# First expert's rows placed by products instead of fetched by index: a decoder layer with two-level expert routing on one core

## The chip, the core and the metric

One core of a Trainium2 chip runs the whole kernel. The metric is the device time of one execution in microseconds (us). Everything is float32. Tiles have 128 partitions (rows of tokens, or slices of the model width). TensorE is called PE below, its weight loads PEld, VectorE DVE, ScalarE ACT, GpSimd POOL, and SyncE SP (it issues the weight transfers).

## The reference, cut to what matters

One layer on 512 prompt tokens and 64 sample tokens (576 rows of width 1024): conditioning, a mixing sub-layer (attention and a gating MLP, one output projection), then the expert sub-layer. Only the seam between the last two is touched:

```
x  = x + ga1 * rms_norm(mix @ w_out, g_post_mix)
h2 = rms_norm(x, g_pre_ffn) * (1 + sc2) + sh2                # 576 x 1024
g_logits = h2 @ w_rg + b_rg                                  # 4 groups: the largest wins
e_logits = h2 @ w_re + b_re                                  # 4 experts in it: the two largest win
y = sum over the 16 experts e of gate[:, e] * (silu(h2 @ w_gate[e]) * (h2 @ w_up[e])) @ w_down[e]
x = x + ga2 * rms_norm(y, g_post_ffn)
```

## The kernel before, in words

The stage that matters is `merge`, followed by `experts`. `merge` goes over five token tiles, in the order `ORDER`: four of 128 prompt rows (tiles 0 to 3) and one of 64 sample rows (tile 4). Before, the order is 0, 1, 2, 4, 3. For each tile PE multiplies the turned mix by the output projection (L2011, two halves of 512 columns; L2019 for the sample tile); ACT sums squares of the result; POOL makes the reciprocal root (L1603 to L1606 for the last tile); DVE adds to x (L1841, L1843 for the last tile), ACT and POOL do the same for the second norm, and DVE makes the normed rows `h2` (L1848, L1849). ACT stores `h2` in memory (L1673, L1691). PE turns `h2` and multiplies it by the router's 20 columns (L1985). The last tile's logits are made from `x` itself, turned (L2038) and multiplied by pre-scaled router columns (L2049), so that they need not wait for `h2`.

Routing is done on DVE by `route(t0, t1)` for the tiles t0 to t1-1: a chain of short instructions (L1749 to L1770), each waiting for the one before. Tiles 0 to 2 are routed while PE still multiplies the last tile; tiles 3 and 4 (the function is called with 3 and 5) come after the last tile's logits. PE counts, for each chosen expert, the rows ahead of each row (`RANK`, products with a triangular and an all-ones matrix: L1969 to L1973 for three tiles, L2054 to L2057 for two). The function `first` turns the ranks for expert 0 into a one-hot matrix `first_row` that says which place each token takes in expert 0's tile of 128 rows. PE multiplies that by the token numbers (L2043, L2061), DVE casts the result into an index list (L1876), and POOL issues an indirect transfer that gathers 128 rows of `h2` from memory (`gather(0)`, L2179). PE turns them (L2322, the function `tokens`), ACT and DVE copy them out of PSUM (L2202, L2079), and the first expert begins.

Each expert is a gate product (L2350, 16 passes of PE over 512 columns), an up product (L2360, 16 passes), the turn of its hidden rows (L2415) and, one expert later, a down product (L2385). PE's order there is gate(e), up(e), tokens(e+1), down(e-1), turn(e). All other lists of rows come from `table` (L2332), which PE runs between gate(0) and up(0) and for which DVE must have finished a long chain (L1877 to L1920); its result is cast at L1922, and POOL then issues `gather(1)` and `gather(2)`. The weights live in a ring of eight slots of 2 MB that SP fills in order; a slot is free again once PE has used it. Expert 0's three and expert 1's gate weights are requested before `merge` begins, expert 1's up and down weights once the output projection is done (L1482), all later ones after DVE has sorted the experts by load (L1924 to L1928, `order_done`).

Of the kernel before, what the change touches and what calls it, by code (L numbers as in the profile page):

```python
# [56 lines left out]
ORDER = (0, 1, 2, 4, 3)  # L57
# [13 lines left out]
def rows(t):  # L71

    return P if t < 4 else NS
# [149 lines left out]
class Program:  # L223
# [1262 lines left out]
    def merge(self, block):  # L1486
# [20 lines left out]
        hv = [L.at(L.V + D * i, D) for i in range(2)]  # L1507
# [27 lines left out]
        both = hot_all[:, 160:256]  # L1535
# [20 lines left out]
        first_row = L.at(L.HT, NT * P).rearrange("p (t c) -> p t c", t=NT)  # L1556
# [23 lines left out]
        def _(sp):  # L1580
# [7 lines left out]
            self.load_expert(sp, 1, 1, 0)  # L1588
            sp.wait_ge(proj_done, 4)
            self.load_expert(sp, 1, 1, 1)  # L1590
            self.load_expert(sp, 1, 1, 2)

        @block.gpsimd
        def _(pool):
            link = chain(pool, pchain, self.pool_count)
            for i, t in enumerate(ORDER):
                n = rows(t)
                for s, first, ready, done in ((ss1, ss1a, sq1, rs1), (ss2, ss2a, sq2, rs2)):
                    pool.wait_ge(ready, i + 1)
                    if i < END:  # L1600
                        self.power(pool, link, s[:, t:t + 1], 1, n, 1.0 / D, done)
                    else:
                        link(pool.tensor_scalar(first, first, 1.0, D * EPS, ALU.mult, ALU.add))  # L1603
                        pool.wait_ge(ready, i + 2)
                        link(pool.tensor_scalar(s[:, t:t + 1], s[:, t:t + 1], first, 1.0 / D, ALU.add, ALU.mult))
                        pool.tensor_tensor(s[:, t:t + 1], s[:, t:t + 1], L.cst("half", n)[:, 0:1], ALU.pow  # L1606
                                           ).then_inc(done, 1)
                if i == 1:
                    pool.wait_ge(ss_ready, 1)
                    self.power(pool, link, ss8, H, NS, 1.0 / DV, ss_power)  # L1610

        @block.scalar
        def _(act):
# [26 lines left out]
            act.dma_start(self.x1[:, 0, :], x_of[0]).then_inc(x_in[0], 16)  # L1640
# [3 lines left out]
            for t in range(1, NT):  # L1644
# [10 lines left out]
            for i, t in enumerate(ORDER[:END]):  # L1655
# [5 lines left out]
                if i >= 2:  # L1661
                    act.wait_ge(h2_tr, i - 1)
                    act.wait_ge(h2_out2[i % 2], 16 * (i // 2))
                act.activation(hv[i % 2][0:n], proj(i, n), ACT.Square, accum_out=ss1[0:n, t:t + 1]).then_inc(sq1, 1)
# [5 lines left out]
                act.activation(hv[i % 2][0:n], self.x1[0:n, t, :], ACT.Square,  # L1670
                               accum_out=ss2[0:n, t:t + 1]).then_inc(sq2, 1)
                act.wait_ge(h2_done, i + 1)
                act.dma_start(self.h2[P * t:P * t + n, :], hv[i % 2][0:n]).then_inc(h2_out2[i % 2], 16)  # L1673
# [1022 lines left out]
```

## Time and profile before

| what | value |
|---|---|
| three runs | 880.01, 882.63, 885.31 us; median 882.63 us |
| the profiled execution | 884.13 us, of which the span of all instructions is 882.4 us |
| PE busy | 811.1 us, 92% of the span |
| mean granted clock of PE | 0.964 of 2.4 GHz |
| last output projection product ends | 534.5 us after the start of the span |
| first expert's gate product begins | 559.28 us |

The span is the time from the first instruction to the last; 1.7 us lie around it. Times of instructions are counted from the start of the span. A line number names a line of the kernel before; where a number of the changed kernel is meant, the text says so. A product in float32 appears as two records ("passes") for each matmul; a turn (transpose) as one. A granted clock of 1.00 is 2.4 GHz, one of 0.50 is 1.2 GHz.

### The profile page before, as it was taken

The numbers are of one execution on the slowest core, as the hardware profiler recorded it, in microseconds if no ns is written. First come the engines' busy times: TensorE is split into PE (matmuls) and PEld (weight loads), VectorE is DVE, ScalarE is ACT, GpSimd is POOL, SyncE is SP. The second block draws the span as 40 slices with busy tenths as digits, with TensorE's granted clock in tenths as the row PEclk, the third lists the DMA queues.
The fourth block names the chain that finished last, engine by engine and source line by source line (L and its number), as shares of the span: only waits on it lengthen the run. The fifth ranks groups of instructions, "written<-read, shape, count | busy, mean of one in ns | idle before, by whom it ended". The sixth has DMA issues, their size and how long they took to land. (4 is left out here: it accounts for less than half of the span.)

```text
span 882.4 us, 12191 instructions
## 1 busy us (share of the span) xinstructions
PE 811.1 (92%) x4728; PEld 411.1 (47%) x4728; DVE 341.6 (39%) x839; ACT 200.2 (23%) x425; POOL 120.5 (14%) x192
## 2 busy tenths in 40 slices
PE   4599999999999999999788987799999999999994
PEld 3144344444446666665544555444444444444431
DVE  3213162346668755555414675510031011110146
ACT  4001000244455433433202111111011110110132
POOL 2220010300002222221101101100000000000044
PEclk8899999999999999999999987799999999999998
DMA  8998194740005979996989515198889999999882
GB/s 295 392 275 355 64 414 136 269 148 2 13 13 209 378 303 425 424 428 283 405 309 329 222 36 215 34 401 330 336 318 408 423 392 426 393 393 387 328 276 107
DMA packets 37142, 249.18 MB, mean 282 GB/s; under 512 B 4809, under 2 KB 6217, under 8 KB 23650
## 3 DMA queue, kind: packets, MB, share of 16 engines
q1 hardware_dynamic: 23490, 156.35, 45.3%
q0 software_dynamic: 9376, 81.47, 23.6%
q10 hardware_dynamic: 4224, 10.65, 3.8%
q8 instruction: 35, 0.57, 0.3%
q14 instruction: 17, 0.14, 0.0%
HBM read 231.92 MB, written 16.53 MB: 282 GB/s over the span
## 5 line engine op out<-in xcount | busy, mean ns | idle before, releaser
L2360 PE MATMUL ps<-sb 128*128 128x512 f32 (+1 forms) x256 | 112.9, 594 | 0.0
L784 PE MATMUL ps<-sb 128*128 128x512 f32 x192 | 86.4, 604 | 1.8 <-DVE sb L442 1.8
L2284 DVE TENSOR_TENSOR sb<-sb,ps 128x512 f32<-128x512 f32 (+1 forms) x16 | 10.9, 684 | 160.3 <-PE ps L2360 87.1
L2350 PE MATMUL ps<-sb 128*128 128x512 f32 x144 | 65.8, 611 | 1.0 <-ACT sb L2202 0.9
L1161 PE MATMUL ps<-sb 128*128 128x128 f32 x512 | 62.9, 276 | 1.8 <-ACT sb L1260 1.8
L2011 PE MATMUL ps<-sb 128*128 128x512 f32 x128 | 59.1, 622 | 4.8 <-ACT sb L1619 2.8
L2385 PE MATMUL ps<-sb 128*128 128x512 f32 x144 | 63.5, 594 | 0.0
L1161 PEld LDWEIGHTS ps<-sb 128*128 128x128 f32 x512 | 55.4, 140 | 13.3 <-issue 10.0
L1064 PE MATMUL ps<-sb 128*128 128x512 f32 x128 | 59.2, 597 | 0.3 <-DVE sb L969 0.3
L2360 PEld LDWEIGHTS ps<-sb 128*128 128x128 f32 (+1 forms) x256 | 42.0, 167 | 34.0 <-issue 34.0
L784 PEld LDWEIGHTS ps<-sb 128*128 128x128 f32 x192 | 36.2, 193 | 45.5 <-issue 43.9
L2357 PE MATMUL ps<-sb 128*64 128x512 f32 x112 | 49.6, 595 | 0.0
L1303 DVE COPY sb<-ps 128x512 f32<-128x512 f32 x64 | 41.2, 686 | 21.6 <-PE ps L1161 21.6
L2179 POOL DMA_INDIRECT sb<-h_rows,ints x16 | 15.0, 940 | 238.6 <-PE ps L2322 209.5
L943 ACT ACTIVATE sb<-sb 128x128 f32<-128x128 f32 (+3 forms) x64 | 35.4, 554 | 52.4 <-DVE sb L1027 52.4
L2350 PEld LDWEIGHTS ps<-sb 128*128 128x128 f32 x144 | 27.4, 195 | 33.1 <-issue 31.2
L2011 PEld LDWEIGHTS ps<-sb 128*128 128x128 f32 x128 | 25.2, 200 | 35.8 <-issue 32.7
L1027 DVE CUSTOM_DVE_ANT_0 sb<-ps,sb 128x128 f32<-128x128 f32 (+3 forms) x64 | 28.8, 488 | 32.9 <-PE ps L1099 29.3
L2385 PEld LDWEIGHTS ps<-sb 128*128 128x128 f32 x144 | 26.7, 190 | 30.3 <-issue 30.1
L2295 DVE COPY sb<-ps 128x512 f32<-128x512 f32 (+1 forms) x16 | 11.1, 692 | 75.8 <-PE ps L2385 56.2
L1260 ACT ACTIVATE sb<-ps 128x512 f32<-128x512 f32 x64 | 34.7, 592 | 21.8 <-PE ps L1161 19.8
L1400 PE MATMUL ps<-sb 128*32 128x512 f32 (+1 forms) x320 | 36.6, 530 | 2.5 <-DVE sb L1347 1.6
(346 smaller groups left out, 1036.2 us busy)
## 6 DMA issues: line engine op xcount, KB each, us to landing
sb<-in_w_gate SPq DMA_DIRECT2D x16, 2048.0 KB, 19.5
sb<-in_w_up SPq DMA_DIRECT2D x16, 2048.0 KB, 9.7
sb<-in_w_down SPq DMA_DIRECT2D x16, 2048.0 KB, 14.3
sb<-in_w_ada SPq DMA_DIRECT2D x12, 2048.0 KB, 18.8
sb<-in_w_in SPq DMA_DIRECT2D x5, 2048.0 KB, 22.1
y_rows<-sb SPq DMA_DIRECT2D x9, 512.0 KB, 15.5
sb<-in_w_out SPq DMA_DIRECT2D x2, 2048.0 KB, 24.2
sb<-in_x_prompt SPq DMA_DIRECT2D x4, 512.0 KB, 5.4
```

What stands on the lines that cost most here:

```text
L784: last = pe.matmul(PS[:, n % 4, :], L.hT[:, k, t * P:t * P + P], w[:, k, :], start=k == 0, stop=k == KC - 1)
L943: act.activation(pb[n % 3][j][:, 0:w], pb[n % 3][j][:, 0:w], ACT.Exp, bias=nm[:, q:q + 1], scale=-1.0, accum_out=sums[:, q:q + 1]).then_in ...
L1064: last = pe.matmul(PS[:, bank, :], L.hT[:, k, t * P:t * P + P], w[:, k, :], start=k == 0, stop=k == KC - 1)
L1161: last = pe.transpose(self.PS[:, h, P * g:P * g + P], kp[:, 4 * (ch % 2) + g, P * h:P * h + P], self.L.cst("ident"))
L1260: act.activation(kt[ch % 2][:, h, :], PS[:, h, :], ACT.Copy).then_inc(kt_act, 1)
L1303: dve.tensor_copy(kt[ch % 2][:, h, :], PS[:, h, :]).then_inc(kt_dve, 1)
L1400: last = pe.matmul(bank[32 * h:32 * h + 32, 0:512 if ch < 4 else NS], qst[par][:, h, :], rhs, start=True, stop=True)
L2011: last = pe.matmul(PS[:, proj_bank(i, c), :], mixT[i % 2][:, k, :], w[:, k, :], start=k == 0, stop=k == KC - 1)
L2350: last = pe.matmul(PS[:, 0, :], x[:, k, :], w_gate[:, k, :], start=k == 0, stop=k == KC - 1)
L2357: last = pe.matmul(PS[n:P, 0, :], x[:, k, :], w_gate[:, k, :], start=k == 0, stop=k == KC - 1)
L2360: last = pe.matmul(PS[0:n, 1, :], x[:, k, :], w_up[:, k, :], start=k == 0, stop=k == KC - 1)
L2385: last = pe.matmul(PS[:, 5 + c, :], hT[:, k, :], w[:, k, 512 * c:512 * c + 512], start=k == 0, stop=k == FC - 1)
```

## The change

Five things are done together.

1. The order of the tiles becomes 1, 2, 3, 4, 0. Tiles 1, 2, 3 are routed together while PE multiplies the last tile's projection, and the sample tile (4) by itself right after them. Only tile 0 is left for the chain behind the last logits; with one tile several pairs of instructions in `route` become one. For that the sample tile's turn, its logits and the ranks of tiles 1 to 3 are put in among the last tile's projection products on PE.
2. Expert 0's rows are no longer gathered. The normed rows of all five tiles stay on chip (in the ring slot of expert 1's gate weights, and one more buffer), and PE multiplies each by its placing matrix `first_row` (the new function `choose_rows`): 8 products of 128 columns for each tile, added up in two PSUM banks that are first set to zero by two products with zero weights. The sum is expert 0's input, already turned. For this the places of expert 0 are now counted from tile 1 on, with tile 0 last.
3. What is gathered by ranks is now expert 1's rows: a second one-hot matrix `second_row` (640 columns), five products with the token numbers, one cast, `gather(1)`.
4. `table` moves from between gate(0) and up(0) to between gate(1) and up(1); its first row list is then expert 2's. The sort of the experts (`order_done`) moves ahead of the long chain on DVE.
5. Expert 1's gate weights are requested after the last placing product, as their slot holds the normed rows until then. The last tile's `h2` is made by a product with the scale first and then one instruction with the reciprocal root, in place of the root first.

The diff, cut to its core:

```diff
-ORDER = (0, 1, 2, 4, 3)
+ORDER = (1, 2, 3, 4, 0)
@@ merge
-        hv = [L.at(L.V + D * i, D) for i in range(2)]
+        held = expert_slot(1, 0)[0]
+        hv = [L.ring[held][:, D * i:D * i + D] for i in range(NT - 1)] + [L.at(L.V, D)]
@@ merge, SP
             for kind in range(3):
                 self.load_expert(sp, 0, 0, kind)
-            self.load_expert(sp, 1, 1, 0)
             sp.wait_ge(proj_done, 4)
             self.load_expert(sp, 1, 1, 1)
             self.load_expert(sp, 1, 1, 2)
+            for out in h2_out2:
+                sp.wait_ge(out, 32)
+            sp.wait_ge(self.x_tr, self.up(self.x_tr, 1))
+            self.load_expert(sp, 1, 1, 0)
@@ merge, DVE
-            route(0, 3)
+            route(1, 4)
+            link(dve.tensor_reduce(three, both[:, 16:64]..., AX, ALU.add))
+            read_logits(END - 1)
+            route(4, NT)
+            dve.tensor_tensor(four, three, both[:, 64:80], ALU.add).then_inc(hot_done, 1)
+            first(1, 4, 1)
...
-            read_logits(i - 1)
-            first(0, 3)
-            dve.wait_ge(rs2, NT)
+            first(4, NT, 2)
             dve.wait_ge(x1_done, NT + 1)
-            link(dve.scalar_tensor_tensor(h, x1, ss2[:, t:t + 1], mod[1], ALU.mult, ALU.mult))
-            dve.tensor_tensor(h, h, mod[2], ALU.add).then_inc(h2_done, 1)
+            link(dve.tensor_tensor(h, x1, mod[1], ALU.mult))
+            dve.wait_ge(rs2, NT)
+            dve.scalar_tensor_tensor(h, h, ss2[:, t:t + 1], mod[2], ALU.mult, ALU.add).then_inc(h2_done, 1)
...
-            route(3, NT)
+            route(0, 1)
...
+            first(0, 1, 3)
+            dve.tensor_copy(ranks[:, 16:96], RANK[:, 16:96]).then_inc(rank_read, 1)
+            dve.tensor_copy(ranks[:, 0:16], RANK[:, 96:112]).then_inc(rank_read, 1)
+            link(dve.scalar_tensor_tensor(rk.unsqueeze(2), rank[:, :, 1:2], 1.0, hot[:, 2, :, 1:2], ALU.add, ALU.mult))
+            dve.scalar_tensor_tensor(second_row, L.cst("row")..., 1.0, rk..., ALU.add, ALU.is_equal).then_inc(first_done, 1)
...
-            dve.tensor_copy(self.ints[:, 0:1], PS[:, 0, 0:1]).then_inc(self.first_ready, 1)
+            dve.tensor_copy(self.ints[:, 1:2], PS[:, 7, 200:201]).then_inc(self.first_ready, 1)
@@ merge, PE
+            def choose_rows(i, ks):
+                t = ORDER[i]
+                n = rows(t)
+                if i == END:
+                    pe.wait_ge(h2_done, NT)
+                for k in ks:
+                    last = pe.matmul(PS[:, 4 * (k // 4), (k % 4) * P:(k % 4) * P + P], hv[i][0:n, k::KC],
+                                     first_row[0:n, t, :], start=False, stop=i == END and k % 4 == 3)
+                return last
...
+                            if (i, f, k) == (END, 1, 2):
+                                logits_of(END - 1)
+                            if (i, f, k) == (END, 1, 4):
+                                ranks_of_three()
                         if i == END and f == 0:
                             last.then_inc(halves, 1)
+                            h2_tr_of(END - 1)
...
-            pe.wait_ge(first_done, 1)
-            for t in range(3):
-                pe.matmul(PS[:, 0, 0:1], first_row[:, t, :], L.cst("token")[:, t:t + 1], start=t == 0, stop=False)
...
+            choose_rows(1, range(KC))
+            choose_rows(2, range(KC))
+            pe.wait_ge(first_done, 2)
+            choose_rows(3, range(KC))
+            pe.wait_ge(hot_done, 4)
+            pe.matmul(RANK[:, 96:112], L.cst("before"), both[:, 0:16], start=False, stop=False)
+            pe.matmul(RANK[:, 80:96], L.cst("ones"), both[:, 0:16], start=False, stop=True).then_inc(rank_done, 1)
+            pe.wait_ge(first_done, 3)
+            choose_rows(END, range(KC)).then_inc(self.x_tr, 1)
+            pe.wait_ge(first_done, 4)
+            for t in range(NT):
+                last = pe.matmul(PS[:, 7, 200:201], second_row[0:n, t, :], L.cst("token", n)[:, t:t + 1],
+                                 start=t == 0, stop=t == NT - 1)
@@ experts, POOL
+            pool.wait_ge(x_tr, self.up(x_tr, 1))
-            gather(0)
+            gather(1)
             pool.wait_ge(self.table_done, 1)
-            for e in range(1, MAIN):
+            for e in range(2, MAIN):
@@ experts, PE
-                if e == 0:
+                if e == 1:
                     table()
...
-            tokens(0, 0, P)
```

PE around the last tile's second projection half, before. L2011 is the projection, L1961 the sample tile's turn, L1969 to L1973 the ranks of three tiles, L1985 the sample tile's logits, L2038 the turn of the last tile's x:

```order
L2011 MATMUL ps<-sb 128x512 [waits e_x1]
L2011 MATMUL ps<-sb 128x512 x7
L1961 MATMUL ps<-sb 128x64 [waits e_h2_ev_dve,e_h2_ev,e_h2]
L1961 MATMUL ps<-sb 128x64 x7
L1969 MATMUL ps<-sb 128x48 [waits e_hot]
L1970 MATMUL ps<-sb 128x32
L1971 MATMUL ps<-sb 128x16
L1973 MATMUL ps<-sb 128x48 x3
L1985 MATMUL ps<-sb 64x20 [waits e_h2_ev_dve,e_h2_ev]
L1985 MATMUL ps<-sb 64x20 x7
```

The same place in the changed kernel, where L2043 is the projection, L1986 the turn, L2017 the logits, and L1994 to L1996 the ranks:

```order
L1986 MATMUL ps<-sb 128x64 [waits e_h2_ev_dve,e_h2_ev,e_h2]
L1986 MATMUL ps<-sb 128x64 x7
L2043 MATMUL ps<-sb 128x512 [waits e_x1]
L2043 MATMUL ps<-sb 128x512 x2
L2017 MATMUL ps<-sb 64x20 [waits e_h2_ev_dve,e_h2_ev]
L2017 MATMUL ps<-sb 64x20 x7
L2043 MATMUL ps<-sb 128x512 x2
L1994 MATMUL ps<-sb 128x48 [waits e_hot]
L1995 MATMUL ps<-sb 128x32
L1996 MATMUL ps<-sb 128x16
L2043 MATMUL ps<-sb 128x512 x3
```

What stood behind the projection now stands inside it, ahead of its last products.

PE from the last tile's logits to the first expert's gate product, before (L2049 the logits, L2054 to L2057 the ranks of two tiles, L2061 the index list, L2322 the turn of the gathered rows, L2350 the gate product):

```order
L2049 MATMUL ps<-sb 64x20 [waits e_h2_ev]
L2049 MATMUL ps<-sb 64x20 x7
L2054 MATMUL ps<-sb 128x32 [waits e_hot]
L2055 MATMUL ps<-sb 128x32
L2057 MATMUL ps<-sb 128x16
L2061 MATMUL ps<-sb 128x1 [waits e_first]
L2061 MATMUL ps<-sb 128x1
L2313 UNCONDITIONAL_BRANCH
L2322 MATMUL ps<-sb 128x128 [waits vs_out]
L2322 MATMUL ps<-sb 128x128 x7
L2350 MATMUL ps<-sb 128x512 [waits ring_full4,ident_in,half_set]
```

The same in the changed kernel (L2093 the logits, L2006 the placing products, L2102 and L2103 the ranks of tile 0, L2109 the index list, L2401 the gate product):

```order
L2093 MATMUL ps<-sb 64x20 [waits e_h2_ev]
L2093 MATMUL ps<-sb 64x20 x7
L2006 MATMUL ps<-sb 128x128 x16
L2006 MATMUL ps<-sb 128x128 [waits e_first]
L2006 MATMUL ps<-sb 128x128 x7
L2102 MATMUL ps<-sb 128x16 [waits e_hot]
L2103 MATMUL ps<-sb 128x16
L2006 MATMUL ps<-sb 128x128 [waits e_h2,e_first]
L2006 MATMUL ps<-sb 128x128 x7
L2109 MATMUL ps<-sb 128x1 [waits e_first]
L2109 MATMUL ps<-sb 128x1 x4
L2365 UNCONDITIONAL_BRANCH
L2401 MATMUL ps<-sb 128x512 [waits ring_full4,cols_in,cols_tr]
```

24 placing products now stand between the logits and the ranks, 8 more and the index list behind them; the gather and the turn of its rows are gone.

## Rows read from the trace of the kernel before

**Rows 1.** Waits of PE, 470 to 560 us: total, times, longest
```profile
PE ps L2054 <- DVE sb L1770: 5.0, 1, 5.0
PE ps L2322 <- DMA sb<-h_rows,ints: 4.9, 1, 4.9
```
**Rows 2.** Chain that ended last, 541 to 578 us: start, us, what
```profile
542.38 1.22 DVE sb L1849
...
543.79 0.17 DVE sb L1754
...
552.09 4.29 DMA sb<-h_rows,ints
...
556.42 1.98 PE ps L2322 x8
...
559.28 8.92 PE ps L2350 x16
...
570.44 7.06 PE ps L2360 x16
```
**Rows 3.** Windows: busy PE, PEld, DVE, ACT, POOL, granted clock, DMA share, GB/s
```profile
534.50:539.00 4.50, 4.18 (x41) 3.83 (x40) 3.02 (x5) 1.79 (x5) 1.17 (x3) 1.00 0.77 255
539.00:541.40 2.40, 2.15 (x12) 2.12 (x12) 1.24 (x5) 1.78 (x4) 1.07 (x3) 0.51 1.02 437
559.28:563.00 3.72, 3.72 (x5) 1.66 (x6) 3.30 (x8) 1.04 (x1) 0.00 (x0) 0.51 0.00 0
580.00:858.00 278.00, 276.26 (x921) 121.61 (x920) 41.26 (x86) 36.02 (x64) 21.02 (x22) 0.99 0.95 374
```
**Rows 4.** Timeline of PE at the projection's end: start, us, engine, line, records
```profile
534.43 1.09 PE L1961 MATMUL ps<-sb 64*128 64x64 f32 x8
536.15 0.85 PE L1973 MATMUL ps<-sb 128*128 128x48 f32 x6
537.96 0.72 PE L2038 MATMUL ps<-sb 128*128 128x128 f32 x4
540.16 1.28 PE L2043 MATMUL ps<-sb 128*128 128x1 f32 x6
541.37 1.90 PE L2049 MATMUL ps<-sb 128*64 128x20 f32 x32
```
**Rows 5.** Timeline of ACT and DVE: a wait, last evacuation, end of routing, one-hot matrix
```profile
535.56 0.42 DVE L1715 COPY sb<-ps 128x256 f32<-128x256 f32 x1 [7.91 <-PE ps L1961]
539.86 1.15 ACT L1688 ACTIVATE sb<-ps 128x512 f32<-128x512 f32 x2
548.01 0.19 DVE L1770 TENSOR_TENSOR sb<-sb 128x32 f32<-128x32 f32 x1
549.96 0.43 DVE L1781 SCALAR_TENSOR_TENSOR sb<-sb 128x256 f32<-128x256 f32 x1
```
**Rows 6.** Timeline: eight turns of 128 columns at clock 1.00
```profile
577.35 1.04 PE L2322 MATMUL ps<-sb 128*128 128x128 f32 x8
```
**Rows 7.** Timeline of DVE: first and last of the table's chain, and of the sort
```profile
551.72 0.16 DVE L1877 TENSOR_SCALAR sb<-sb 128x16 f32<-128x16 f32 x1
558.49 0.69 DVE L2079 COPY sb<-ps 128x512 f32<-128x512 f32 x1 [0.96 <-PE ps L2322]
562.68 0.10 DVE L1920 MEMSET sb<- 64x52 f32 x1
570.58 0.42 DVE L1924 TENSOR_TENSOR sb<-sb 128x256 f32<-128x256 f32 x1
573.38 0.17 DVE L1936 CAST ints<-sb 128x11 int32<-128x11 f32 x1
```
**Rows 8.** Gathers of `h2` rows issued at 570.94, 572.22 and 578.66: us to landing
```profile
DMA to landing us min/median/max: 4.2/11.4/11.7
```
**Rows 9.** Weight transfers of SP: first of two at 534.5, last of four at 577.7
```profile
DMA to landing us min/median/max: 7.9/7.9/7.9
DMA to landing us min/median/max: 24.7/24.7/24.7
```

More of the change, by code:

```diff
@@ L1506, in merge @@
         sq = L.at(L.QKT + 4096, 512, 0, NS)
-        hv = [L.at(L.V + D * i, D) for i in range(2)]
+        held = expert_slot(1, 0)[0]
+        hv = [L.ring[held][:, D * i:D * i + D] for i in range(NT - 1)] + [L.at(L.V, D)]
+        squares = [L.at(L.V + D + 512 * i, 512) for i in range(2)]
+        rank_read = self.later("rank_read")
         osb = L.at(L.V + 2048, 512, 0, NS)
@@ L1534, in merge @@
         hot = hot_all[:, 0:240].rearrange("p (j t e) -> p j t e", j=3, t=NT)
-        both = hot_all[:, 160:256]
+        both = hot_all[:, 160:240]
+        three, four = hot_all[:, 240:256], take("four", NE)
         prod = take("prod", 80).rearrange("p (t e) -> p t e", t=NT)
@@ L1595, in _ @@
             link = chain(pool, pchain, self.pool_count)
-            for i, t in enumerate(ORDER):
+            for i, t in enumerate(ORDER[:END]):
                 n = rows(t)
-                for s, first, ready, done in ((ss1, ss1a, sq1, rs1), (ss2, ss2a, sq2, rs2)):
+                for s, ready, done in ((ss1, sq1, rs1), (ss2, sq2, rs2)):
                     pool.wait_ge(ready, i + 1)
[L1600 to L1607, printed above, removed]
+                    self.power(pool, link, s[:, t:t + 1], 1, n, 1.0 / D, done)
                 if i == 1:
@@ L1610, in _ @@
                     self.power(pool, link, ss8, H, NS, 1.0 / DV, ss_power)
+            t = ORDER[END]
+            for s, first, ready, done in ((ss1, ss1a, sq1, rs1), (ss2, ss2a, sq2, rs2)):
+                pool.wait_ge(ready, NT)
+                link(pool.tensor_scalar(first, first, 1.0, EPS, ALU.mult, ALU.add))
+                pool.wait_ge(ready, NT + 1)
+                link(pool.tensor_scalar(s[:, t:t + 1], s[:, t:t + 1], first, 1.0, ALU.add, ALU.mult))
+                pool.tensor_tensor(s[:, t:t + 1], s[:, t:t + 1], L.cst("half")[:, 0:1], ALU.pow).then_inc(done, 1)
         @block.scalar
@@ L1643, in _ @@
             act.dma_start(mod[2], row_of(3)).then_inc(mod_in, 16)
-            for t in range(1, NT):
+            for t in ORDER[1:]:
                 act.dma_start(self.x1[0:rows(t), t, :], x_of[t]).then_inc(x_in[t], 16)
@@ L2027, in _ @@
                     mix_tr(i + 1)
-                else:
-                    ranks_of_three()
-                if i >= 1:
+                if 1 <= i < END:
                     logits_of(i - 1)
+            pe.wait_ge(first_done, 1)
+            pe.wait_ge(hot_done, 3)
+            pe.matmul(RANK[:, 64:80], L.cst("before"), both[:, 64:80], start=True, stop=False)
+            pe.matmul(RANK[:, 64:80], L.cst("ones"), three, start=False, stop=True)
+            pe.matmul(RANK[:, 80:112], L.cst("ones"), four.unsqueeze(1).to_broadcast([P, 2, 16]),
+                      start=True, stop=False).then_inc(rank_done, 1)
+            for b in (0, 4):
+                pe.matmul(PS[:, b, :], L.cst("sameseq")[NS:P, 0:1].to_broadcast([P - NS, P]),
+                          L.cst("ident")[NS:P].unsqueeze(1).to_broadcast([P - NS, 4, P]), start=True, stop=False)
+            choose_rows(0, range(4))
             pe.wait_ge(h2_ev, END)
@@ L2040, in _ @@
                 last.then_inc(h2_tr, 1)
[L2041 to L2043 removed]
+                if f == 0:
+                    choose_rows(0, range(4, KC))
             pe.wait_ge(log_read, END)
```

147 lines of the change are left out of this document (76 added, 71 removed).

## The prediction, made before the changed kernel was run

> **What bounds the kernel now.** I read the busy shares in long windows first. From 580 to 858 us PE is busy 276.26 of 278.00 us at a granted clock of 0.99 [rows 3]: the experts are a plain stream of products, and no transfer, copy or other engine is waited for there. The change leaves the number and size of those products as they are, so it can move the end only by moving the start of that stream or by opening a hole in it. The waits of PE before it come next: between 470 and 560 us it waits 5.0 us for the end of routing (L1770) and 4.9 us for the gathered rows [rows 1]. The chain that ended last tells what lies between: the end of the last tile's `h2` (L1849, to 543.60), routing from 543.79, the gather at 552.09 (4.29 us), eight turns (1.98 us), their copy out of PSUM, the gate product at 559.28 [rows 2]. Last I looked at the clock. It fell at 539.0 us, although PE was busy 4.18 of the 4.50 us before, with turns and narrow products; it stayed at 1.2 GHz through the routing and came back at 563.0, after 3.7 us of products 512 columns wide [rows 3]. The first gate product therefore takes 8.92 us where the up product takes 7.06 [rows 2]: 1.9 us lost.
>
> **The change part by part**, in times of the profiled execution. Its span is 882.4 us, its own time 884.13, and it ran 1.50 us above the median of the three runs; I make the sum against 884.13 and take 1.50 off at the end.
>
> *The projection ends later.* The sample tile's turn, the ranks of three tiles and the logits stand inside the projection. Before they ran from 534.43 to 537.96, with 0.77 us for L1973, whose 0.85 us overlap the next record a little and which goes [rows 4]: 3.53 - 0.77 = +2.7 us. Their inputs are early, so no wait is added. Everything behind (squares, root, the sum with x, the turned x) moves by the same 2.7 us, as the chain ACT, POOL, DVE was what ran there and these products lay beside it.
>
> *The last logits and `h2`.* L2043 (1.28 us), which held up the logits before, is gone from there. ACT's evacuation ended at 541.01 [rows 5], now 543.7; the second half of the logits' 1.90 us [rows 4] follows it: 544.7 to 545.2. In `h2` the product with mod[1] goes ahead of the root, which takes the 1.22 us of one full-width instruction [rows 2] off the path: 543.60 + 2.7 - 1.2 = 545.1. Both meet at 545.2, and routing starts at 545.6, against 543.79: +1.8.
>
> *Routing one tile.* From L1754 at 543.79 to the end of L1770 at 548.20 there are 22 instructions [rows 2, 5], 0.20 us each. For one tile there are 18: 3.6 us, so they end at 549.2. The first three tiles and the sample tile are routed under the projection: DVE waited 7.91 us there, until 535.56 [rows 5]. The sample tile's logits arrive at about 532.5, its 19 instructions, one sum and `first` end near 537.4, and DVE's next work is at 539. That costs nothing.
>
> *The placing products are the new last wait.* Each is two passes of 128 columns, and the trace of before has none. Two rows bound a pass at full clock: a quarter of a 512-column pass (7.06 / 16 / 4 = 0.110 us) [rows 2] and a turn (1.04 / 8 = 0.130 us) [rows 6]; I take 0.122, between them, since both the columns and the weight load must fit in. At 1.2 GHz a turn takes 1.98 / 8 = 0.247 us [rows 2]. Setting the two banks to zero is 4 passes of 0.44 = 1.8 us, and tile 1's products 2.0 us: with the turned x they fill PE from 537.4 to 543.0, beside the root and the sums, and delay nothing by more than 0.2. From 545.2 PE has three tiles, 48 passes, 5.9 us: until 551.1. Routing ended at 549.2. So PE, not DVE, is late by 1.9 us. The bounds are 550.5 and 551.4. Then two rank products (0.5 us, by the 0.85 us for six passes [rows 4] and the latency of one) and `first` for 128 columns (0.45, by 0.43 for 256 columns and 0.16 for the short one ahead [rows 5]): 552.1.
>
> *From there to the gate product.* The last tile's 16 passes, 2.0 us, then the index list's 10 passes, which stand ahead of the gate product on PE: 1.28 us for six at 1.2 GHz [rows 4] makes 0.21 each there, about 0.11 at full clock, 1.1 us. The copies out of PSUM (0.88 us, from 558.40 to 559.28 [rows 2]) lie beside them. The gate product starts at 555.3, against 559.28: -4.0 us. At full clock it takes 7.0 us and not 8.92: -1.9.
>
> *DVE behind it.* The table's chain was 551.72 to 562.78, with 1.57 us for the copy L2079 and the wait ahead of it; the sort and the overflow list 570.58 to 573.55 [rows 7]. Now all of this (9.5 + 3.0 = 12.5 us) stands ahead of expert 0's hidden rows. It starts 4.4 us after `first` (two copies, the 640-column one-hot matrix at 0.83, four short ones, x out of PSUM 0.69, the ordering of experts 1.1) and ends 16.9 us after it; the up product ends 3.2 + 14.0 = 17.2 after it. They meet; I take +0.3 for the crowding there.
>
> *Table.* It costs the same between gate and up of either expert: 0 (the 2 us between the gate product's end and the up product's start at 570.44 [rows 2] are paid once in both). Gather(1) is issued some 4.7 us after `first` and used 17.2 after it; a gather took 4.2 to 11.7 us [rows 8], so it is just hidden. Gather(2) follows the table and has the 6.5 us of one up product, as gather(1) had before, when it landed in 4.2 us. Expert 1's gate weights are asked for at 554.2 and used at about 571; alone such a transfer takes 7.9 us [rows 9]. The earlier requests of experts 2 and 3 bring nothing, as nothing waited for weights.
>
> Sum: -4.0 - 1.9 + 0.3 = -5.6 us, 878.5 in the profiled execution's terms, 877.0 against the median.
>
> **Two rules of the Trainium skill.** The rows give 0.110 to 0.130 us for a pass of 128 columns with its weight load. The skill ("TensorE: Matmul & The Clock Gate", section "Back-to-back issue gap") measures about 81 ns for such a pair in a stream. By it 48 passes would take 3.9 us and not 5.9; no row here is so short, and the turns [rows 6] speak against it. What comes of it as a mechanism is the second case below. A gather that starts while weights are moving took 11.4 or 11.7 us, one that starts on quiet engines 4.2 [rows 8]. The skill's "DMA: Bandwidth & Descriptors", section "Issuing engines are not separate DMA queues", says transfers of all issuing engines interleave on the same 16 engines; the trace agrees, and that speaks against the table's new place, since more weights are then on their way: the fourth case.
>
> **The rivals.**
> (1) *As summed*: 877.0, with 875 to 879.5 as its own range. 42%.
> (2) *Short passes.* If a placing pass takes 0.08 us, PE is done at 549.1, routing is last at 549.2, and the last tile's 16 passes take 0.7 us less: 1.9 + 0.7 earlier, less about 0.8 as DVE's chain then ends last. 875.3. For it: placing products have no wait among them. Against: the turns [rows 6]. 8%.
> (3) *The clock falls on the way.* Turns and logits between 541 and 545 are the kind of work at whose end it fell before [rows 3]. The 48 passes that follow bring it back, but a stretch of 3.5 us at 1.2 GHz costs about 1.8 us; one or two of them make 878.8 to 880.5, say 879.5. 25%.
> (4) *A gather is late.* Gather(2) starts behind the table while the fifth weight transfer since 554 may still run: five of 2.1 MB at the 374 to 437 GB/s seen [rows 3] are 24 to 28 us, so they last until 578 to 582, and the gather starts near 580.5. If it took 11.5 us and not 6.5, PE stands for up to 5.0 us; half of that on average: 879.5. For it: the landings [rows 8]. Against: the transfers should be nearly through. 13%.
> (5) *Slower: the half clock holds through the placing products.* If they do not bring the clock back, the work from 537.4 to the gate product is 80 placing passes of 0.21 to 0.247 us, 3.5 us for the zeros, 2.0 for turns, 1.9 for logits, 2.4 for ranks, 2.1 for the index list and about 1 us of waits: 30 to 33 us, and the gate product starts 8 to 11 us later than before. With 1.9 back if the clock is up by then, that is 888.7 to 891.7, say 890. It decides once the clock is low at 541 and stays low: above about 4.5 us of delay the gain is gone. Against: wide products lifted the clock at 563.0. 7%.
> (6) *Expert 1's gate weights come late.* Asked for last and sharing the way with expert 2's, they might take the 24.7 us of the last of four transfers [rows 9] and not the 16.8 there are: +7.9, 884.9. Against: they go first in their queue. 5%.
>
> **How the numbers follow.** 0.5% of 882.63 is 4.4 us, about what a measurement of this kernel can tell from none. Faster by more means below 878.2: 0.75 of case 1, nearly all of 2, 0.3 of 3 and of 4, in sum 0.49. Slower by more means above 887.0: case 5 and a part of 6, 0.08. Within: 0.43. The range runs from 873.5 (case 2 with passes and copies at their shortest) to 884.5, which takes in 3 and 4 and leaves 5 and most of 6 out.
>
> **What would show it.** Right: no gather ahead of the first expert; the gate product about 18 us after the last projection product ends (24.8 before) and at a granted clock of 1.00; PE without a hole from the last logits to the ranks, which wait for nothing; routing ended about 2 us before that. Wrong: a granted clock of 0.50 within the placing products (3 or 5), PE waiting for routing (2), a wait of the turns of expert 1 or 2 for gathered rows (4), of the second gate product for weights (6), or of the first turn of hidden rows for DVE by more than 0.5 us, which would mean that I made the chain on DVE too short.

## The result, and the profile after

The changed kernel takes 889.75 us (median of 9 runs, 887.71 to 891.80); the kernel before took 883.32 beside it (9 runs). The ratio is 1.0069, 95% interval 1.0053 to 1.0086: slower by 0.7%, where I had forecast 877.0 and gave "slower" 8 in 100. The profiled execution of after took 888.19 us with a span of 886.4, and is read here against the one of before (span 882.4).

I look first for what I said would show each step. PE's waits between 540 and 600 us are down to one, of 0.6 us; the two of 5.0 and 4.9 us [rows 1] are gone. DVE waits for PE instead:

```profile
PE ps L2006 <- DVE sb L1798: 0.6, 1, 0.6
```

And DVE's largest waits in the same stretch:

```profile
DVE ints L2342 <- PE ps L2383: 9.5, 1, 9.5
DVE sb L1795 <- PE ps L2103: 8.4, 1, 8.4
```

The second of these is the finding. L1795 is `first` for the last tile on the routing chain, which waits for the ranks (L2103), and these stand on PE behind the placing products (L2006). DVE's chain was done early and stood for 8.4 us. The timeline of PE from the last pieces of the projection to the up product (start, us, engine, line, records), to set beside [rows 4] and the chain [rows 2]:

```profile
529.78 1.09 PE L1986 MATMUL ps<-sb 64*128 64x64 f32 x8
...
533.58 1.11 PE L2017 MATMUL ps<-sb 128*64 128x20 f32 x16
...
537.02 2.82 PE L2043 MATMUL ps<-sb 128*128 128x512 f32 x6
...
540.78 1.98 PE L2075 MATMUL ps<-sb 64*128 64x512 f32 x4
542.69 2.17 PE L2006 MATMUL ps<-sb 128*128 128x128 f32 x8
544.70 0.60 PE L2083 MATMUL ps<-sb 128*128 128x128 f32 x4
545.13 2.07 PE L2006 MATMUL ps<-sb 128*128 128x128 f32 x8
547.04 0.60 PE L2083 MATMUL ps<-sb 128*128 128x128 f32 x4
547.57 1.40 PE L2093 MATMUL ps<-sb 128*64 128x20 f32 x32
548.90 11.98 PE L2006 MATMUL ps<-sb 128*128 128x128 f32 x48
...
562.43 4.09 PE L2006 MATMUL ps<-sb 128*128 128x128 f32 x16 [0.58 <-DVE sb L1798]
566.35 1.26 PE L2109 MATMUL ps<-sb 128*128 128x1 f32 x10
567.54 7.13 PE L2401 MATMUL ps<-sb 128*128 128x512 f32 x16
```

A placing pass takes 11.98 / 48 = 0.250 us, not 0.122. All other rows are about what I had taken: four turns in 0.60 us, ten passes of the index list in 1.26, the gate product 7.13 instead of 8.92. The windows say whether it was the clock (columns as in [rows 3]):

```profile
545.00:559.00 14.00, 13.89 (x89) 13.52 (x87) 6.25 (x25) 1.99 (x6) 1.29 (x2) 1.00 0.60 233
559.00:567.60 8.60, 8.02 (x39) 7.66 (x38) 3.04 (x13) 1.03 (x2) 0.00 (x0) 0.60 0.03 8
580.00:858.00 278.00, 277.14 (x970) 124.05 (x969) 41.37 (x93) 34.13 (x63) 22.20 (x23) 1.00 0.93 367
```

It was not: until 559 us the granted clock is 1.00, the higher level, and the passes are slow there too. It fell to 0.50 at 559.0, within the placing products and ahead of any wait, and rose again at 565.9. That cost little: the last 16 placing passes took 4.09 us, 0.256 each, nearly all of them at the lower level, and the two rank products with the wait behind them about 0.4 us more than in e1 below. The second column of busy times points to the weight loads: PEld is busy for 13.52 of 14.00 us, where in [rows 3] it is under half of PE's in the streams of wide products. By itself this says only that the passes are narrow. What is new is the length of the load's record, a median of 335 ns, where the projection's, contiguous, have 190 (duration ns min/median/max):

```profile
L2006 PEld LDWEIGHTS ps<-sb x80: 309/335/338, 542.7 to 566.0; 128*128 128x128 f32 x64, 64*128 64x128 f32 x16
L2043 PEld LDWEIGHTS ps<-sb x128: 186/190/338, 451.0 to 538.8; 128*128 128x128 f32 x128
```

The first gate product starts 27.7 us after the last projection product (537.02 + 2.82 = 539.84 to 567.54), where I expected 18 and before had 24.8. Behind it the kernel is as it was: no wait for rows or weights, 277.14 busy us of 278.

A difference to keep in mind: the profiled pair differs by 4.1 us, the medians by 6.4. The first projection product of all began 1.6 us later in this execution of after (L2043 at 451.0, before L2011 at 449.4), before anything that the change slows. At the last expert's down products the pair is 6.5 us apart (842.80 and 849.26), and before then loses 2.5 of it again in its tail: PE waits 1.7 us there for DVE against 0.8, and the products behind that wait ran in part at the lower level of the clock, in before and then in after:

```profile
848.76 5.35 PE L2390 MATMUL ps<-sb 128*64 128x512 f32 x16 [1.74 <-DVE sb L2295]
```

```profile
854.24 3.65 PE L2443 MATMUL ps<-sb 128*64 128x512 f32 x16 [0.76 <-DVE sb L2347]
```

Single executions of a kernel scatter by several us. So below I compare the distance from the last projection product to the first gate product, which this does not touch, and use medians only with their intervals.

### The profile page after: what moved, and what is told of

It reads as the page before. It is cut to its first block, busy times and chain, and to the rows that moved or that the text cites. A ratio compares the mean times of both kernels' runs of the same rounds, so it can differ in the third digit from the quotient of the medians.

```text
span 886.4 us, 12365 instructions
## 1 busy us (share of the span) xinstructions
PE 829.9 (94%) x4802; PEld 426.0 (48%) x4802; DVE 346.2 (39%) x861; ACT 200.3 (23%) x426; POOL 119.1 (13%) x191
## 4 chain that ended last, share of the span: by engine, by line
PE 72%; DMA 12%; DVE 6%; issue 3%; POOL 2%; ACTq 2%; ACT 1%; SPq 1%; POOLq 0%; DVEq 0%
PE ps L784 10%; DMA sb<-in_cache_v,ints 8%; PE ps L2401 7%; PE ps L2413 7%; PE ps L2438 7%; PE ps L1064 6%; PE ps L2043 5%; PE ps L2410 5%; DMA sb<-in_w_ada 3%; PE ps L1440 3%; PE ps L1161 2%; PE ps L2006 2%; PE ps L2443 2%; PE ps L541 2%; PE ps L1099 2%
## 5 line engine op out<-in xcount | busy, mean ns | idle before, releaser
L2333 DVE TENSOR_TENSOR sb<-sb,ps 128x512 f32<-128x512 f32 (+1 forms) x16 | 10.9, 684 | 149.3 <-PE ps L2413 76.1
L2043 PE MATMUL ps<-sb 128*128 128x512 f32 x128 | 60.6, 630 | 5.2 <-ACT sb L1629 3.2
L2401 PE MATMUL ps<-sb 128*128 128x512 f32 x144 | 64.0, 597 | 0.1
L2043 PEld LDWEIGHTS ps<-sb 128*128 128x128 f32 x128 | 25.2, 201 | 35.4 <-issue 31.8
L2401 PEld LDWEIGHTS ps<-sb 128*128 128x128 f32 x144 | 26.7, 190 | 30.8 <-issue 30.1
```

Of the source, the lines that this page charges most:

```text
L2043: last = pe.matmul(PS[:, proj_bank(i, c), :], mixT[i % 2][:, k, :], w[:, k, :], start=k == 0, stop=k == KC - 1)
L2401: last = pe.matmul(PS[:, 0, :], x[:, k, :], w_gate[:, k, :], start=k == 0, stop=k == KC - 1)
```

## The experiments

*The theory.* A placing product reads its stationary operand as every eighth column of the normed rows (`hv[i][0:n, k::KC]`, elements 32 bytes apart). The weight load of such an operand in an ordinary float32 product takes 0.25 us whatever the clock; contiguous, it would take 0.12 at full clock and the forecast would have held. *The rival.* An ordinary float32 product 128 columns wide always pays its load and its stream one behind the other, 0.125 + 0.125 us, and the stride is innocent. Two smaller ones: something of the moving operand or of the place in the program; and that the rest of the change (routing of one tile, order of tiles) is what costs.

**e1_contiguous.** One line of after, which leaves expert 0's input with its columns in another order:

```diff
-  last = pe.matmul(PS[...], hv[i][0:n, k::KC], first_row[0:n, t, :], ...)
+  last = pe.matmul(PS[...], hv[i][0:n, k * P:k * P + P], first_row[0:n, t, :], ...)
```

> The kernel after, with the stationary operand of the 80 placing passes (L2006) read as 128 neighbouring columns of hv instead of every eighth one; expert 0's input then has its columns in another order, all work is otherwise the same. The stride theory: the weight load of a strided float32 operand sets the 0.25 us of a pass; contiguous, a pass takes 0.11 to 0.13 us as the index list's passes do (1.26 us for 10). The last logits' placing work (48 passes) ends about 7 us earlier, the first gate product starts at about 559.4 us instead of 567.5, the time is 881.5 us (880 to 883). The rival, that load and stream of any 128-column float32 product stand one behind the other: the pass stays at 0.25 us and the time at 889.8 us.

Measured: 876.70 us, ratio to before 0.9907 (0.9872 to 0.9943). The timeline of PE again:

```profile
548.11 5.82 PE L2006 MATMUL ps<-sb 128*128 128x128 f32 x48
...
555.05 2.05 PE L2006 MATMUL ps<-sb 128*128 128x128 f32 x16 [0.57 <-DVE sb L1798]
556.94 1.26 PE L2109 MATMUL ps<-sb 128*128 128x1 f32 x10
558.13 7.13 PE L2401 MATMUL ps<-sb 128*128 128x512 f32 x16
```

The pass takes 0.121 us, and the gate product starts 18.7 us after the projection's last product (539.44), 9.0 us sooner than in after. The rival is out. Even here the clock was low for a while, from 542.4 to 545.8 us, and the first eight contiguous passes took 0.245 us each in it; without that the distance is about 17.6 us, as e5 and e6 below have it:

```profile
542.28 1.96 PE L2006 MATMUL ps<-sb 128*128 128x128 f32 x8
```

The medians moved by 13 us, 5 more than I expected of it, and the profiled pair by 9.9; I come back to that.

**e2_narrow.** The moving operand cut from 128 to 32 columns, the strided stationary one kept (three quarters of expert 0's rows are left out):

```diff
-  PS[:, 4 * (k // 4), (k % 4) * P:(k % 4) * P + P], hv[i][0:n, k::KC], first_row[0:n, t, :]
+  PS[:, 4 * (k // 4), (k % 4) * P:(k % 4) * P + 32], hv[i][0:n, k::KC], first_row[0:n, t, 0:32]
```

> The kernel after, with 32 instead of 128 moving columns in each placing product (96 of 128 rows of expert 0's input are left at zero); the stationary operand stays strided. The stride theory (the weight load alone sets the pass): a pass stays at 0.25 us. The rival (load and stream one behind the other): 0.125 for the load and 0.03 for the stream, 0.155 us a pass, and the gate product starts some 6 us earlier than at 567.5.

Measured: 891.07 us, one run. The first eight placing passes ran at a granted clock of 1.00 and start 0.24 us apart with a quarter of the columns (1.93 us from the first to the next product on PE, for 8): the load alone sets the pass.

```profile
540.30 2.09 PE L2006 MATMUL ps<-sb 128*128 128x32 f32 x8
542.23 1.08 PE L2083 MATMUL ps<-sb 128*128 128x128 f32 x4
...
547.70 11.75 PE L2006 MATMUL ps<-sb 128*128 128x32 f32 x48
```

The 48 passes take 11.75 / 48 = 0.245 us each, but the window over them shows the clock at the lower level all along. A contiguous pass of 128 columns takes 0.24 there too (e1 above), so these 48 alone would not have told the two theories apart. What they do show is that the strided passes are no slower at this level than at the higher one in after.

```profile
547.70:559.30 11.60, 11.60 (x50) 11.54 (x48) 3.81 (x22) 0.42 (x2) 0.00 (x0) 0.50 0.26 96
```

**e4_stride4 and e5_stride2.** The same operand read with strides of 4 and of 2 elements (expert 0's input then has its columns in another order):

```diff
-  hv[i][0:n, k::KC]
+  hv[i][0:n, k // s * 128 * s + k % s : k // s * 128 * s + k % s + 127 * s + 1 : s]    # s = 4, s = 2
```

> The kernel after, with the placing products' stationary operand read with a stride of 4 elements (16 bytes) instead of 8 (expert 0's input then has its columns in another order). If the loss sets in once each element lies in a piece of 16 bytes of its own, a pass takes 0.25 us as with 8 elements; if it grows with the stride, about 0.19 us; if only strides above 16 bytes lose, 0.125 us. The rival theory, without any stride effect: 0.25 us.

> The kernel after, with the placing products' stationary operand read with a stride of 2 elements (8 bytes). With 4 elements (16 bytes) a pass took 0.245 us, with 8 the same, with 1 0.121. If what counts is how many elements share a piece of 16 bytes, two do here and the pass takes 0.121 to 0.13 us; if any stride loses, 0.245 us.

The records of L2006 in the two, first stride 4, then stride 2 (duration ns min/median/max of PEld, the weight load):

```profile
L2006 PEld LDWEIGHTS ps<-sb x80: 305/329/332, 539.5 to 562.4; 128*128 128x128 f32 x64, 64*128 64x128 f32 x16
```

```profile
L2006 PEld LDWEIGHTS ps<-sb x80: 192/196/197, 540.0 to 553.4; 128*128 128x128 f32 x64, 64*128 64x128 f32 x16
```

Stride 4 costs as much as stride 8 (48 passes in 11.76 us, 0.245 each; 884.85 us), stride 2 next to nothing (6.12 us, 0.128 each; 875.24 us, one run each). The gate product starts 27.3 and 17.6 us after the last projection product, against 27.7 in after; that e4's single time lies 5 us under after's median is not explained by its passes. So the price is the same for 16 and 32 bytes; it sets in at some stride above 8 bytes and at most 16.

The Trainium skill has a passage on this ("SBUF — State Buffer", section "Door 1: The DMA port swizzle"): memory lines of 16 bytes, which need two hits or more each for full bandwidth. It adds that one can stride "for free" over 4 fp32. The first sentence agrees with these rows, 0.128 us with two elements in 16 bytes and 0.245 with one; the second, read as a stride of 4 elements, does not, for a stride of exactly 4 costs as much as one of 8. That the lines are the cause is argued from this agreement; the runs show the price, not the reason. The prediction did not weigh this page.

**e13_turn_by_product.** Why, then, did the turns mislead me, which read the same rows with the same stride in 0.130 us a pass [rows 6]? The router's turns of after, made as ordinary products on the same operands:

```diff
-  last = pe.transpose(PS[...], hv[i][0:n, k::KC], L.cst("ident", n)[:, 0:n])
+  last = pe.matmul(PS[...], hv[i][0:n, k::KC], L.cst("ident", n)[:, 0:n], start=True, stop=True)
```

> The kernel after, with the turns of the normed rows for the router (L1986) made by ordinary float32 products with the identity instead of by transposes, on the same operand with the same stride of 8 elements: twice as many passes, since such a product goes in two. If it is the ordinary float32 product whose weight load suffers from the stride, a pass takes 0.245 us, as the placing passes do, where a transpose's takes 0.130; a tile's turn goes from 1.04 to 3.9 us, and the time grows by 5 to 11 us. If the placing passes are slow for another reason (their moving operand, their place in the program), a pass here takes 0.12 to 0.13 us.

Measured: 896.27 us, one run. A tile's turn goes from 1.04 us in 8 passes to 3.84 in 16, 0.240 each, at a granted clock of 1.00:

```profile
503.49 3.84 PE L1986 MATMUL ps<-sb 128*128 128x128 f32 x16
```

Same rows, same stride, another place: the ordinary float32 product pays, the transpose does not. In e3_ordered, below, where the transposes read contiguously, eight still take 1.04 us.

**e3_ordered.** The whole reference computed, with the normed rows stored in the order in which they are turned; VectorE writes them with the stride. Done also in the last tile and in the gathered tiles:

```diff
-  link(dve.scalar_tensor_tensor(h, x1, ss2[0:n, t:t + 1], mod[m + 1][0:n], ALU.mult, ALU.mult))
-  dve.tensor_tensor(h, h, mod[m + 2][0:n], ALU.add).then_inc(h2_done, 1)
+  hp = h.rearrange("n (k p) -> n p k", k=KC)
+  nat = lambda a: a.rearrange("n (p k) -> n p k", k=KC)
+  link(dve.scalar_tensor_tensor(hp, nat(x1), ss2[0:n, t:t + 1], nat(mod[m + 1][0:n]), ALU.mult, ALU.mult))
+  dve.tensor_tensor(hp, hp, nat(mod[m + 2][0:n]), ALU.add).then_inc(h2_done, 1)
...
-  B["xg"][par][0:n, k::KC]
+  B["xg"][par][0:n, k * P:k * P + P]
```

> The kernel after, with the normed rows (hv, their store in HBM, and so the gathered rows too) kept in the order in which the turns read them, so that the stationary operand of placing products and of all turns of normed and gathered rows is 128 neighbouring columns; VectorE writes the rows with a stride instead. All of the reference is computed. The stride theory: gate product at about 559.4 us, less 0.2 or so for turns, plus 0 to 2.4 us for strided reads and writes in the last tile's two VectorE instructions: 881.5 us (879.5 to 884). The rival: 889.8 us or more.

Measured: 877.14 us (11 runs), ratio 0.9929 (0.9906 to 0.9952): a complete kernel that beats the one of before by 0.7% and that of after by 1.4%, and 4 us under what I expected of it. The stride is not free on VectorE either. The two instructions of the last tile, 1.22 and 1.28 us in after:

```profile
547.00 1.98 DVE L1875 TENSOR_TENSOR sb<-sb 128x1024 f32<-128x1024 f32 x1
549.74 2.02 DVE L1877 SCALAR_TENSOR_TENSOR sb<-sb 128x1024 f32<-128x1024 f32 x1 [0.77 <-POOL sb L1620]
```

**e6_one_strided_write and e7_strided_reads.** The first of the two instructions now works in natural order into a scratch buffer, and only the second changes the order, by its write or by its reads:

```diff
+  out = lambda a: a.rearrange("n (k p) -> n p k", k=KC)     # e7: "n (k p) -> n k p"
+  nat = lambda a: a.rearrange("n (p k) -> n p k", k=KC)     # e7: "n (p k) -> n k p"
+  link(dve.scalar_tensor_tensor(raw, x1, ss2[0:n, t:t + 1], mod[m + 1][0:n], ALU.mult, ALU.mult))
+  dve.tensor_tensor(out(h), nat(raw), nat(mod[m + 2][0:n]), ALU.add).then_inc(h2_done, 1)
```

> As e7_strided_reads, but the second instruction reads in natural order and writes with the stride. The second instruction of the last tile takes 2.0 us as in e3_ordered, the first 1.22; the gate product starts about 19.0 us after the last projection product.

> As e3_ordered, all of the reference computed, but of the two VectorE instructions that make a tile's normed rows the first works in natural order on contiguous rows, and the second reads with a stride of 8 elements and writes contiguously. If only strided writes of VectorE lose (1.98 us against 1.22 in e3_ordered's last tile), both instructions of the last tile take 1.2 to 1.3 us, PE's wait of 1.0 us for the end of routing (L2106 on L1787 in e3_ordered) goes, and the first gate product starts 18.7 us after the last projection product, as in e1_contiguous (19.8 in e3_ordered): 876 us. If a strided read costs the same as a strided write, 18.7 to 19.1 us and 876.5.

The second instruction took 2.02 us with the strided write and 2.08 with strided reads: the guess that only writes lose is wrong. Measured: 874.27 us (one run) and 878.16 us (7 runs, ratio 0.9927, 0.9900 to 0.9953), the latter no better than e3. Their profiles show why single executions of these kernels lie apart. PE from the ranks on, in e6 and then in e7:

```profile
553.43 2.05 PE L2010 MATMUL ps<-sb 128*128 128x128 f32 x16 [0.57 <-DVE sb L1798]
555.31 1.26 PE L2113 MATMUL ps<-sb 128*128 128x1 f32 x10
556.50 7.13 PE L2405 MATMUL ps<-sb 128*128 128x512 f32 x16
```

```profile
553.21 3.04 PE L2010 MATMUL ps<-sb 128*128 128x128 f32 x16 [0.58 <-DVE sb L1798]
556.04 2.21 PE L2113 MATMUL ps<-sb 128*128 128x1 f32 x10
558.18 10.16 PE L2405 MATMUL ps<-sb 128*128 128x512 f32 x16
```

In e7 the granted clock fell to 0.51 at about 554 us, behind PE's waits around the ranks, and stayed low into the products of expert 0: 1.0 + 1.0 + 3.0 us in these three rows. It also fell behind the same waits in the profiled executions of e3 and of e12 below. But waits are neither needed nor enough. In after, e4 and e13 it fell at 559.0, 555.3 and 568.0 us while PE ran strided placing passes without a hole, and in e1 it had fallen at 542.4, while PE waited for nothing; in e5 and e6, with waits of 0.58 and of 0.28 and 0.57 us around the ranks, it stayed at 1.00 from 530 to 580 us. This is my third case, the clock that falls on the way: about 1.1 us in e1, where it fell at the place I had named, and 3.3 us (e3) to 5.0 (e7, e12) behind the ranks, where I had said 1.8 a time.

**e9_no_zeros.** e6, without the two products that set the banks to zero:

```diff
-  for b in (0, 4):
-      pe.matmul(PS[:, b, :], L.cst("sameseq")[NS:P, 0:1].to_broadcast([P - NS, P]), ..., start=True, stop=False)
-  ... start=False, stop=i == END and k % 4 == 3)
+  ... start=i == 0 and k % 4 == 0, stop=i == END and k % 4 == 3)
```

> As e6_one_strided_write (all of the reference computed), and without the two products that set banks 0 and 4 to zero (1.98 us of PE): the first placing product of each bank starts it instead. PE has no hole between the projection and the last logits in e6_one_strided_write but 0.39 us, and the logits there wait for the root anyway, so of the 1.98 us only about 0.5 to 1 can be gained, and after it routing (ended 0.28 us after PE there) is last: the gate product starts 17.5 to 18.0 us after the last projection product (17.57 there, by 556.50 less 538.93), 0 to 0.3 us earlier; the time is 875 to 877 us, not to be told from e6's. The rival, that PE's amount of work sets the end: -2.0 us.

Measured: 877.89 us (6 runs), ratio 0.9931 (0.9903 to 0.9958). The 1.98 us turned into a wait of PE of 1.55 us for the halves of x1 (L1871), and the gate product starts 18.2 us after the projection's last one, 0.6 later than in e6, for the clock fell in that wait, at 544.6: the eight contiguous placing passes that follow took 1.91 us, 0.24 each. Nothing gained, and the rival, 2 us less by less work on PE, is out.

**e12_root_first.** e1, with the last tile's `h2` in the old order, the root first:

```diff
-  link(dve.tensor_tensor(h, x1, mod[1], ALU.mult))
   dve.wait_ge(rs2, NT)
-  dve.scalar_tensor_tensor(h, h, ss2[:, t:t + 1], mod[2], ALU.mult, ALU.add).then_inc(h2_done, 1)
+  link(dve.scalar_tensor_tensor(h, x1, ss2[:, t:t + 1], mod[1], ALU.mult, ALU.mult))
+  dve.tensor_tensor(h, h, mod[2], ALU.add).then_inc(h2_done, 1)
```

> As e1_contiguous (expert 0's input in another column order), but in the last tile's normed rows the product with mod[1] waits for the root as before. If PE is the last to come (by 1.8 us in e1_contiguous, where VectorE waited 1.77 us for the ranks), the 1.2 us vanish: the gate product starts 18.7 us after the last projection product as there. If VectorE's chain were last, 19.9.

Measured: the gate product starts 19.6 us after the projection (884.01 us, one run). But the low clock took 1.9 of that from the last 16 placing passes (3.02 us) and the index list (2.21). Without it, it is 17.7, as in e5 and e6, so nearly all of the 1.2 us of the reordering was hidden. I had compared with e1, whose PE was late by its own spell of low clock; at full clock PE and VectorE are about level, and here PE waits 0.41 us for routing.

**e8_gather and e11_gather_2.** After with expert 0's rows gathered and turned as before, everything else of the change kept. In e8 I had put VectorE's copy of the turned rows too late, and PE stood 4.3 us for it; e11 mends most of that.

```diff
-  choose_rows(...)                                  # all placing products, and the two banks set to zero
+  pe.matmul(PS[:, 0, 0:1], first_row[...], L.cst("token")[...], ...)       # expert 0's index list
+  gather(0)
+  tokens(0, 0, P)
```

> The kernel after, but expert 0's rows are gathered by an index list and turned, as before, and no placing products or zeroing stand on PE; one tile alone on the routing chain, the new order of the tiles, the sample tile's products inside the projection, the second expert's list by ranks and the table between expert 1's products stay. By my terms: projection end +2.7, start of routing +1.8, routing 3.9 instead of 4.4 us, and from there 11 us as before, so the gate product starts 0.5 to 1.3 us later than at 559.3 us (25 less 1.5 us after the last projection product) and at 1.2 GHz (8.9 us): 884.5 us (883 to 886), no gain. The rival, that the routing chain and the order of tiles carry a gain of their own: the gate product 2 us or more earlier than before, 881 us or less.

> As e8_gather, but VectorE's copy of expert 0's turned rows stands 2.7 us earlier in its chain. In e8_gather PE stood 4.3 us between the turns (ended 562.85) and the gate product, because that copy came at 566.37 behind the table's chain, which is my placing of it and no part of the changed kernel. Here the gate product should start 24 us after the last projection product (27.2 in e8_gather, 24.8 before): 886 us. If the routing chain and the order of tiles carried a gain of their own it would be 881 or less.

Measured: 889.42 us, ratio 1.0059 (1.0037 to 1.0081), and 888.46 us (10 runs), ratio 1.0051 (1.0020 to 1.0082), 2.5 us above what I expected of the second. Its gate product starts 24.5 us after the projection's last one, against 24.8 before, and runs at the low clock (9.32 us):

```profile
562.75 1.97 PE L2369 MATMUL ps<-sb 128*128 128x128 f32 x8 [1.69 <-DMA sb<-h_rows,ints]
566.77 9.32 PE L2397 MATMUL ps<-sb 128*128 128x512 f32 x16 [2.05 <-issue]
```

The 2.05 us ahead of it are again the copies out of PSUM, VectorE's still late in its chain (565.98 to 566.67); before the change they took 0.9, so about 1.2 us of the 24.5 are my placing. Even with these taken off, the new order, the inserted products and the routing of one tile bring the gate product 1.5 us nearer to the projection's end, less than the 3.0 us by which the inserted products move that end. They give nothing by themselves, and the gain of e1 and e3 comes from placing rows in the gather's stead.

## Why the prediction was wrong

*The step that failed* is "The placing products are the new last wait", in one term: "I take 0.122" for a pass. It measured 0.250 us. I bounded it by a quarter of a 512-column pass, whose stationary operand is contiguous [rows 2], and by a turn, whose operand is strided but which is a transpose [rows 6]. Neither row has both properties of the new product, strided and ordinary, and I called them bounds. The terms that hung on it: 48 passes 12.0 us for 5.9, and the last 16 4.1 for 2.0, in sum 8.2; and the sixteen of tile 1, ahead of the last logits, which held up the turned x by 2 us, for which I had said "delay nothing by more than 0.2", and with it the start of the 48 passes by 1.1 (9.1 us after the projection for 8.0). The fall of the clock at 559.0 added about 0.4 at the ranks. Gate at 27.7 us after the projection for 18.1. That PE and not DVE is late there was right, but by 7.7 us (560.9 against 553.2) and not by 1.9.

*Contiguous, the sum holds.* With the pass at 0.121 us, e1 has the gate product at 18.7 us, e6 at 17.6, for 18.1; the times are 876.70, 877.14 (e3) and 878.16 (e7), for 877.0. By their ratios to the kernel before that is 8.2, 6.3 and 6.4 us less, where I had 5.6. So near a number is in part luck, as spells of low clock that cost 1 to 5 us lie in some of the traces and not in others.

*The other steps*, in the profile of after:
- Inserted products: between the first 16 projection passes (end 529.85) and the last (539.84) lie 10.0 us for 7.0 us of wide products, so 3.0 for 2.7. Right.
- Routing one tile: 549.29 to 553.23, 3.94 us for 3.6; each of the 18 takes 0.22, not 0.20, as forms with a scalar read from memory (0.22 to 0.23) replace some of 0.17. Hidden by PE.
- Gate product at full clock: 7.13 for 7.0. Right.
- DVE's chain meets the up product: L2333 waits for it 0.27 us in after and 0.28 in e1. Right, and so close that a longer chain would show.
- Table, gathers, weights: no wait. Rivals 4 and 6 did not occur.

*The rivals.* The time was that of case 5 (890), "Slower: the half clock holds through the placing products", but not by its mechanism: the clock was at 1.00 through the first 10.1 us, some 40 of the 48 passes. Its price, 0.247 us a pass, was right by chance, for the strided load takes that at either level. Its sign, a clock of 0.50 within the placing products, did appear at 559.0, so that sign alone would have misled. Case 2, short passes, is refuted by 0.121 us. The Trainium skill's 81 ns for a pair ("TensorE: Matmul & The Clock Gate", section "Back-to-back issue gap") is met by no stream of 128-column passes here. Case 3 exists, at 1.1 us in e1 and about 5 in e7.

*Open.* From after to e1 the distance to the gate product shrinks by 9.0 us and the profiled spans by 9.9, but the medians by 13.1. The missing 3.2 us are where the profiled executions lie among their own: that of after is 1.6 us under its median, that of e1 1.6 over. Likewise e11 lies 11.8 above e1 where the distances and the gate product account for 8. Spells of low clock of 1 to 5 us and the waits of the tail are seen to differ from trace to trace, but only one execution of each kernel has a trace, so what makes up these 3 to 4 us was not settled. Nor was why the clock falls: it fell behind waits in some traces and in full streams of passes in others.

## What to carry to other kernels

A bound from a neighbouring row holds only if that row shares the property that costs: before you price a new product by an old one, compare operand layout and kind (ordinary or transpose) of both, not only the shape. If a float32 matrix is to be the stationary operand of ordinary products, lay its columns down at most two elements apart, even if another engine must pay for it once where it is hidden: here 0.75 us on each of ten VectorE instructions (e3), most of it hidden (PE waits 1.0 us for the end of routing there), bought 0.13 us at full clock on each of 80 passes. And read the length of the weight load's records beside PE's spacing. That PEld is busy nearly as long as PE does not tell a slow load from a quick one: it was so with strided passes (13.52 of 14.00 us in after) and with contiguous ones (5.55 of 5.80 in e1); the records, 335 ns against 192, do.

```profile
548.10:553.90 5.80, 5.80 (x53) 5.55 (x49) 3.81 (x22) 0.42 (x2) 0.00 (x0) 1.00 0.80 299
```

## What the runs showed of the hardware

- Ordinary float32 product with a stationary operand and a moving one of 128 columns, in a stream at a granted clock of 1.00: 0.121 us a pass contiguous, 0.128 with stride 2, 0.245 with stride 4, 0.250 with stride 8; with 64 rows instead of 128 the same (e13, 4.01 us for 16 passes of the sample tile). With 32 moving columns and stride 8, 0.24 (e2).
- The strided pass took 0.250 us at a granted clock of 1.00 and 4.09 / 16 = 0.256 at the lower level (both in after): it does not follow the clock. The contiguous one does: 0.121 at 1.00, 0.24 at the lower level (e1, e9). So at the lower level the stride costs next to nothing.
- Transposes of float32 do not pay for the stride: 0.130 us a pass at stride 8 and contiguous alike, although the load's own record shortens from 193 ns (after, L1986) to 140 (e3, L1990).
- VectorE, 1024 float32 per row with all operands in SBUF: 1.22 and 1.28 us contiguous, 1.98 to 2.08 with a stride of 8 elements, on the written side or on the read side alike.
